# Eight-core decoder layer: inputs and output laid out feature-major by the host, next tile normalised inside the last down projection

## What is computed

```
x = x + 1/2 * SwiGLU_1(RMSNorm(x))          # w1, w3: 1024 x 2816, w2: 2816 x 1024
h = RMSNorm(x); x = x + mixer(h)            # w_in 1024 x 5648, gated linear attention, pooling, merge
x = x + CrossAttention(RMSNorm(x), RMSNorm(mem))
x = x + 1/2 * SwiGLU_2(RMSNorm(x))
out = RMSNorm(x)
rmsnorm(x, g) = x * rsqrt(mean(x*x, axis=-1) + 1e-6) * g
swiglu(h) = (silu(h @ w1) * (h @ w3)) @ w2
```

## Time and profile before

| | us |
|---|---|
| median of 3 runs | 3675.35 (3672.68 to 4205.69) |
| span of the profiled execution, slowest core (core 0) | 3676.3 |
| spans of the eight cores in it | 3661.8 to 3676.3 |
| TensorE matmuls busy | 3382.7 (92%) |
| VectorE, ScalarE, GpSimd busy | 1379.5, 916.6, 353.3 |
| DMA, share of 16 engines | 55.6% (weights), 3.1% (x, mem, out) |

### The profile page before, as it was taken

One profiled execution on the slowest core, in us unless ns is written; L12 is line 12 of the kernel. 1 busy time (PEld: TensorE's weight loads), 2 busy tenths in 40 slices (PEclk: granted clock), 3 DMA queues, 4 the chain that ended last, 5 costly groups with the idle time before them and its releaser, 6 DMA issues.

```text
span 3676.3 us, 43383 instructions; the slowest of 8 cores (3661.8 to 3676.3 us)
## 1 busy us (share of the span) xinstructions
PE 3382.7 (92%) x16248; PEld 1581.1 (43%) x16248; DVE 1379.5 (38%) x1860; ACT 916.6 (25%) x1285; POOL 353.3 (10%) x362
## 2 busy tenths in 40 slices
PE   5999799899799969999979997989998999798998
PEld 3444444344444434334444443434444444343444
DVE  2213545622322354552232246463223125546312
ACT  3112332211311332221131144222113114312211
POOL 1111000011111000001101100001110010000110
PEclk9999899999899979999999998999999999899999
DMA  9568247267766633735875853475595584253565
GB/s 165 69 64 105 39 67 125 36 74 71 112 77 67 85 47 59 126 46 62 83 115 62 81 74 45 73 111 61 63 105 89 66 91 68 36 78 49 69 66 90
DMA packets 538363, 282.33 MB, mean 77 GB/s; under 512 B 261280, under 2 KB 523440, under 8 KB 538160
## 3 DMA queue, kind: packets, MB, share of 16 engines
q0 software_dynamic: 523904, 244.49, 55.6%
q1 hardware_dynamic: 14256, 35.06, 3.1%
HBM read 507.21 MB, written 16.78 MB: 143 GB/s over the span
## 4 chain that ended last, share of the span: by engine, by line
PE 84%; DVE 7%; ACT 3%; issue 2%; DMA 2%; DVEq 0%; POOL 0%; ACTq 0%; SPq 0%; POOLq 0%
PE psum_all L103 84%; DVE sb_hT L378 2%; DVE ov_rz_102 L1056 1%; DMA sb_slot<-xa_wv 1%; DVE ov_rz_103 L1056 1%; DMA out<-ov_ost_51 1%; ACT ov_sq L358 1%; PE psum_all L119 1%; DVE ov_ogT L886 1%; DVE sb_xT L378 1%; DVE ov_xo L1062 1%; ACT ov_rsn L879 0%; ACT ov_rsn L878 0%; ACT ov_osq L868 0%; DVE sb_xT L1010 0%
## 5 line engine op out<-in xcount | busy, mean ns | idle before, releaser
L103 PE MATMUL psum_all<-sb_hT,sb_slot 128*128 128x512 bf16 (+1 forms) x8512 | 1896.6, 385 | 37.3 <-DVE sb_hT L378 30.9
L103 PEld LDWEIGHTS psum_all<-sb_hT,sb_slot 128*128 128x128 bf16 (+1 forms) x8512 | 838.7, 99 | 1060.5 <-issue 99.8
L103 PE MATMUL psum_all<-ov_gated,sb_slot 128*128 128x512 bf16 x2816 | 611.2, 379 | 0.0
L131 POOL DMA_DIRECT2D sb_slot<-ffn_w x264 | 272.3, 1036 | 2099.2 <-PE psum_all L103 2062.4
L103 PEld LDWEIGHTS psum_all<-ov_gated,sb_slot 128*128 128x128 bf16 x2816 | 275.7, 98 | 332.9 <-issue 2.6
L358 ACT ACTIVATE ov_sq<-sb_xT 128x2048 bf16<-128x2048 f32 x80 | 148.4, 1902 | 944.6 <-DVE sb_xT L501 533.1
L486 DVE TENSOR_TENSOR ov_gated<-psum_all,ov_sl_55 128x512 bf16<-128x512 f32 x176 | 121.7, 691 | 478.5 <-PE psum_all L103 478.5
L486 DVE TENSOR_TENSOR ov_gated<-psum_all,ov_sl_54 128x512 bf16<-128x512 f32 x176 | 121.6, 691 | 460.9 <-PE psum_all L103 411.0
L501 DVE SCALAR_TENSOR_TENSOR sb_xT<-psum_all,sb_xT 128x512 f32<-128x512 f32 x128 | 88.1, 691 | 455.5 <-PE psum_all L103 455.5
L378 DVE SCALAR_TENSOR_TENSOR sb_hT<-sb_xT,sb_small,ov_rstd 128x512 bf16<-128x512 f32 x256 | 172.4, 746 | 144.3 <-ACT ov_rstd L372 144.3
L483 ACT ACTIVATE ov_sl_55<-psum_all 128x512 bf16<-128x512 f32 x176 | 105.1, 597 | 487.1 <-PE psum_all L103 487.1
(11 more groups left out here) (174 smaller groups left out, 2292.2 us busy)
## 6 DMA issues: line engine op xcount, KB each, us to landing
sb_slot<-ffn_w POOLq DMA_DIRECT2D x176, 512.0 KB, 8.9
sb_slot<-ffn_w POOLq DMA_DIRECT2D x88, 704.0 KB, 9.4
sb_slot<-w_in POOLq DMA_DIRECT2D x44, 1024.0 KB, 11.8
sb_slot<-w_up_a POOLq DMA_DIRECT2D x8, 1024.0 KB, 8.9
sb_slot<-w_mix_out POOLq DMA_DIRECT2D x8, 1024.0 KB, 12.0
sb_slot<-xa_wq POOLq DMA_DIRECT2D x8, 1024.0 KB, 23.5
sb_slot<-xa_wo POOLq DMA_DIRECT2D x8, 1024.0 KB, 21.4
sb_slot<-w_up_b POOLq DMA_DIRECT2D x4, 1024.0 KB, 9.1
```

Source lines behind the costliest of these rows:

```text
L103: ("ins", (lambda e, o=o, l=l, r=r, st=st, sp=sp: e.matmul(o, l, r, start=st, stop=sp)), i == n - 1)
L131: self.prog[queue].append(("dma", (lambda e, o=o, i=i: e.dma_start(out=o, in_=i)), key))
```

## The change

The host function writes x, mem and out feature-major and each slot's weights in the order in which they lie in the slot, so that a slot load is 128 runs of 4096 float32 (2816 for w2) and x can be read into feature-major buffers directly. All float32 transposes of x, mem and out, `load_block`, `store_block`, `boundary`, `ost`, `stg` and `xpf` go. x is read into two chunk buffers `xin` (58 to 90 K); the first norm reads them and writes `hT`, and phase 2 of ffn(0) takes its residual from them. Stores go from `xT` straight to DRAM. Within phase 2 of ffn(1), hooks run the two first norms of the next tile after groups (0,1), (0,2), (0,4) and (0,5) (chunk, m), and the final norm of chunk 0 after (0,7) and (1,6); the final norm of chunk 1 is deferred into the next tile's phase 1. Squares and multiplications of a norm wait for the groups of features that they read, no longer for all eight. `mem_prologue` moves from the start to between ffn(0) and mixer of the first tile.

```diff
-    x_d = din("x", [SEQ, D])
-    mem_d = din("mem", [MEM, D])
+    x_d = din("x", [SEQ // SUB, 128, 8, SUB])
+    mem_d = din("mem", [128, 8, MEM])
...
+    w13_d = [din("ffn1_w13", [NJ // 2, 128, 4096]), din("ffn2_w13", [NJ // 2, 128, 4096])]
+    w2_d = [din("ffn1_w2", [8, 128, NJ * 128]), din("ffn2_w2", [8, 128, NJ * 128])]
+    win_d = din("w_in", [11, 128, 4096])
...
-        S.dma("pool", [(vf(st), src) for (vf, src) in parts], [], [slot_b[i]], f"dma:slot{i}")
+        S.dma("pool", [(st[:, 0:src.shape[1]], src)], [], [slot_b[i]], f"dma:slot{i}")
...
+    def run_hook(hooks, at):
+        if at in hooks:
+            lab = S.label
+            S.label = lab.split("/")[0] + "/tailnorm"
+            for f in hooks[at]:
+                f()
+            S.label = lab
...
-            S.op("dve", lambda e, bk=bk, m=m, s=s: e.scalar_tensor_tensor(
-                out=xT[:, m, s * SUB:(s + 1) * SUB], in0=bk[:], scalar=0.5, in1=xT[:, m, s * SUB:(s + 1) * SUB],
-                op0=ALU.mult, op1=ALU.add), [bb], [xT_b[m][s]])
+            if x_in is None:
...
+            else:
+                S.op("dve", lambda e, bk=bk, m=m, s=s: e.scalar_tensor_tensor(
+                    out=xT[:, m, s * SUB:(s + 1) * SUB], in0=bk[:], scalar=0.5, in1=x_in[s][0][:, m, :],
+                    op0=ALU.mult, op1=ALU.add), [bb, x_in[s][1][m]], [xT_b[m][s]])
+            run_hook(hooks, (s, m))
...
+    def load_chunk(k, step=4):
+        xt, xb = xin[k % 2]
+        for lo in range(0, 8, step):
+            S.dma("sp", [(xt[:, lo:lo + step, :], x_d[k, :, lo:lo + step, :])], [], xb[lo:lo + step], f"dma:x{k % 2}_{lo}")
+
+    def first_norm(c):
+        xt, xb = xin[c]
+        return norm_pieces(lambda lo, hi: xt[:], lambda c_: xb, T, O_G_FFN1, hdst, hdb, c)
+
+    def final_norm(t, c):
+        p_sq, p_ones, p_rest = norm_pieces(xsrc, xbufs, T, O_G_FIN, xsrc, xbufs, c)
+
+        def p_out():
+            for lo in range(0, 8, 4):
+                S.dma("sp", [(out_d[t * NSUB + c, :, lo:lo + 4, :], xT[:, lo:lo + 4, sl(c)])],
+                      [xT_b[m][c] for m in range(lo, lo + 4)], [], f"dma:out{c}_{lo}")
+        return p_sq, p_ones, p_rest, p_out
...
+    S.label = "load"
+    load_chunk(0, 2)
+    ffn_pre(0)
+    load_chunk(1)
+    n0 = first_norm(0)
+    for p in n0:
+        p()
+    n1 = first_norm(1)
+    n1[0]()
+    deferred.extend(n1[1:])
     for t in range(nt):
...
+        last = t + 1 == nt
+        S.label = "ffn0"
+        if t > 0:
             ffn_pre(0)
...
+        nx = norm_pieces(xsrc, xbufs, T, O_G_MIX, hdst, hdb, 0)
+        ffn(0, xin, {(0, 7): [nx[0]], (1, 6): nx[1:]})
+        if t == 0:
+            mem_prologue()
+        mixer(t)
+        xattn()
+        if not last:
+            load_chunk(2 * t + 2)
+            load_chunk(2 * t + 3)
+        S.label = "ffn1"
+        norm_x_to_h(O_G_FFN2, chunks=(1,))
+        fz = final_norm(t, 0)
+        hooks2 = {(0, 7): [fz[0]], (1, 6): fz[1:]}
+        if not last:
+            na, nb_ = first_norm(0), first_norm(1)
+            hooks2.update({(0, 1): [na[0]], (0, 2): na[1:], (0, 4): [nb_[0]], (0, 5): nb_[1:]})
+        ffn(1, None, hooks2)
+        S.label = "store"
+        fy = final_norm(t, 1)
+        fy[0]()
+        deferred.extend(fy[1:])
+        if last:
+            run_deferred()
```

More of the change, by code:

```diff
@@ L244, in build_program @@
     ptmp, ptmp_b = ov("ptmp", 36, [128, 4, SUB], F32)
-    xpf = [ov(f"xpf{i}", 58 + 4 * i, [128, D], F32) for i in range(8)]
+    xin = [ov(f"xin{i}", 58 + 16 * i, [128, 8, SUB], F32, nb=8) for i in range(2)]
     qT, qT_b = ov("qT", 0, [128, 4, T], BF16, nb=8)
@@ L468, in ffn @@
         for pair in pairs:
-            loaded = [wload(ffn_parts(l, jp), key=("ffn", l, jp)) for jp in pair]
+            loaded = [wload(w13_d[l][jp], key=("ffn", l, jp)) for jp in pair]
             for s in range(NSUB):
@@ L631, in load_tile @@
-    def load_tile(t):
-        S.label = "load"
-        pcs = norm_pieces(xsrc, xbufs, T, O_G_FFN1, hdst, hdb, 0) if stage >= 1 else None
-        for blk in range(T // 128):
-            if pcs is not None and blk == 4:
-                pcs[0]()
-            if pcs is not None and blk == 6:
-                pcs[1]()
-                pcs[2]()
-            load_block(blk)
-    def store_tile(t, final_norm=True):
-        S.label = "store"
-        if final_norm:
-            rmsnorm_T(xsrc, xbufs, T, O_G_FIN, xsrc, xbufs, chunks=(1,), defer_last=True)
-        for blk in range(T // 128):
-            store_block(t, blk)
-            if blk == 1:
-                run_deferred()
@@ L695, in mixer @@
         S.label = "mix"
-        winv = kview(win_d)
-        wpre("mix_q", proj_parts(winv[:, :, 0:512], 4, 8))
-        wpre("mix_k", proj_parts(winv[:, :, 512:1024], 4, 8))
+        wpre("mix_q", win_d[0])
+        wpre("mix_k", win_d[1])
         norm_x_to_h(O_G_MIX, chunks=(1,))
@@ L707, in ev_qk @@
                      [kT_b[s * 4 + i] for i in range(4)])
[L708 to L709 removed]
+        proj_multi([(win_d[0], "mix_q"), (win_d[1], "mix_k")], 4, 8, hrhs, hrb, ev_qk)
+        st, sbuf = wload(wa_d)
         sv = v3(st, 8, 16)
@@ L1070, in ev_o @@
                  [bb], [xT_b[mm_][s]])
-        proj_multi([(wov[:, :, half * 512:(half + 1) * 512], None) for half in range(2)], 4, 8,
+        proj_multi([(wo_d[half], None) for half in range(2)], 4, 8,
                    lambda kc, s: xo[:, kc, sl(s)], lambda s: [xo_b[kc * 2 + s] for kc in range(8)], ev_o,
-                   hook=(tail_hook(O_G_FFN2, 8) if stage >= 4 else None))
-    mem_prologue()
-    prefetch_tile(0)
-    load_tile(0)
+                   hook=tail_hook(O_G_FFN2, 8))
+    S.label = "load"
@@ L1100, in build_program @@
+        ffn(1, None, hooks2)
[5 more added lines that the diff above has]
+            run_deferred()
     fin = []
-    for key in [f"dma:out{i}" for i in range(8)]:
+    for key in [f"dma:out{c}_{lo}" for c in range(2) for lo in (0, 4)]:
         if key in S.dmacnt:
@@ L1147 @@
         m = dict(shared)
-        m["x"] = np.ascontiguousarray(inp["x"][b], dtype=np.float32)
-        m["mem"] = np.ascontiguousarray(inp["mem"][b], dtype=np.float32)
+        m["x"] = np.ascontiguousarray(f32(inp["x"][b]).reshape(SEQ // SUB, SUB, 8, 128).transpose(0, 3, 2, 1))
+        m["mem"] = np.ascontiguousarray(f32(inp["mem"][b]).reshape(MEM, 8, 128).transpose(2, 1, 0))
         in_maps.append(m)
     res = run_bass_kernel_spmd(nc, in_maps, core_ids=list(range(8)))
-    out = np.stack([np.asarray(r["out"], dtype=np.float32) for r in res.results], axis=0)
+    out = np.stack([np.asarray(r["out"], dtype=np.float32).transpose(0, 3, 2, 1).reshape(SEQ, D) for r in res.results],
+                   axis=0)
     return out
```

244 lines of the change are left out of this document (67 added, 177 removed).

## The result

The changed kernel takes **3542.3 us** (median of four runs, 3541.9 to 3543.4) against 3675.35 before: the ratio is 0.9641, 95% interval 0.9625 to 0.9658, 3.6% less. The forecast was 3549 us, 3.4% less. Of four runs of the kernel before, two ran at a lowered clock and are left out of the ratio (3672.68 and 3675.35 us are left).

The account below looks back on a forecast made before the run. TensorE matmuls were taken to bound the kernel, with gains only outside dense runs: 3676.3 - 125.2 (boundaries) - 29.5 (start) + 35 (mem) - 6.3 (end) = 3550.3, taken as 3549 us against the median; range 3525 to 3590.

Parts of the forecast that it names:

- the taking of turns: DMA queues alternate packet by packet whatever the row length, so at the start x chunk 0 lands at 31.5 us.
- the mem term: Between first ffn(0) and mixer: mem load 9.3 us, norm 9.9, K and V matmuls 16.6; +35 us, bounds 28 and 47.
- Boundaries: At the three tile boundaries transposes and waits go and only the layer's matmuls stay: 125.2 us saved together.
- The count "92 matmuls stay": At the first tile boundary only 92 needed matmuls remain, 19.9 of 62.5 us; 89 at the other two, 19.2 us.
- Rival 2: A deferred final norm or norms in phase 2 hold up banks, 12 us each time: 3585 us; chance 10%.
- Start: Before the first dense run: x arrives at 31.5 us, first matmul 43.2, run begins 62.8; 29.5 us saved (20 to 45.6).
- End: After the last final norm, direct stores replace transposes, copies and small stores: 6.3 us saved (2 to 8).
- Weights in slot order: Weight packets fall from 523,904 to about 34,300, queue share to 35%; no gain counted beyond the old prologue.
- "The per-group waits of a norm shorten nothing on TensorE": Norms waiting only for the feature groups they read save nothing, since each chunk-0 norm is early already.
- Rivals 3 and 4: 3: long dense runs lower the clock, near 4050 us, 4%. 4: long rows slow per byte, DMA bound, 3760 us, 3%.

Follow-up runs that it names:

- experiment 5: Changed kernel with the next tile's two first norms put back behind phase 2 of ffn(1): 3593.9 to 3626.5 us, ratio 0.9796.
- Experiments 1 and 2: Changed kernel with x chunk 0 in one DMA of 16 KB rows (lowest 3531.6 us); with the first five weight slot loads in 4 KB rows (3529.7 and 3530.6 us).
- experiment 3: Changed kernel with the first weight slot load waiting until x chunk 0 has landed: 3525.6 to 3526.65 us, ratio 0.9595.
- the six runs of experiment 10: The changed kernel twice and experiments 1, 2, 3 and 5, all with whole weight rows beside mem; mem's last row at 4.6 to 6 us on 21 of 48 cores.
- experiment 6: Kernel before the change with only the weights laid out in slot order: lowest 3679.8 us, ratio 1.0017.
- experiment 7: Changed kernel with the weights back in the reference's order, run twice: ratios 0.9696 and 0.9668, against 0.9639 for the changed kernel beside the second.
- experiments 7 and 8: 8 is the changed kernel with the first slot load behind x chunk 0 and mem loaded and normalised inside ffn(0): lowest 3519.9 us, ratio 0.9573.

## Where the prediction held and where it failed, point by point

The total was 7 us off in 3542, and the sign, the mechanism of the boundaries and the taking of turns held. The step that failed is the mem term, the load of mem above all (+41.5 instead of +35), and that the total was closer than this is luck. Each change below is from core 0 before to core 4 after, the two profiled slowest cores.

- **Boundaries** (forecast -125.2): the stretch from the last evacuation of ffn(1) to the next gate code went from 309.3, 306.6 and 309.8 us to 262.65 three times; phase 2 of ffn(1) grew by 3.5 us for the two groups of column sums. Net -43.2, -40.5, -43.7: **-127.4**. The count "92 matmuls stay" was right to 1.2 us each. Rival 2 has nothing: no wait stands in the boundary, and experiment 5 shows what it costs when the norms are behind (52 us).
- **Start** (-29.5): x at 30.9 us against 31.5, first matmul 43.8 against 43.2, run 64.0 against 62.8: **-28.4**. That the queues take turns by row whatever its length was the disputed step. Experiments 1 and 2 each change the length on one side, and both move the start as the turns say; experiment 3 shows only that the weights beside x are what holds it up. The Trainium skill ("DMA: Bandwidth & Descriptors", section "SWDGE vs HWDGE vs iDMA") has packets of at most 4096 B by preference; the measured mean of 7.4 KB a packet and x at 31 us, not 16, decide against it here. The size was luck, though. The sum had the weights begin at 6 us behind two rows of x an engine, then 30 pairs of 0.851 us. On core 4 the first weight row starts at 7.4 us, when 179 of the 512 rows of x (11 an engine) are gone, and the other 333 take 22 us, some 1.05 us for each of 21 turns: fewer turns, and longer ones. By core, the second Square starts at 26.9 to 32.2 us.
- **mem_prologue** (+35): **+41.5** on the slowest core. This is the step that failed: "Eight pairs of 337 + 683 ns ... less the lead of SP over POOL, 9.3 us". Measured are 15.3 us on core 4. The sum had mem beside V's weights and mix_q alone; K's weights, issued before, were not yet through, so SP's lead is none (the first mem row goes 2.2 us after the issue), and from mem's first to its last row it is 10.6 us with 134 weight rows between, 1.32 us for each of eight pairs instead of 1.02. Where K's weights are through, the load takes 5.3 us and the term is +31 to +33, so the 9.3 us are right for neither form. The pause of TensorE before K is 25.6 us on core 4, where 19 were forecast. In this execution only cores 1 and 4 have the long form; over the six runs of experiment 10, it is 22 cores of 48, and the slowest core is the metric. Norm and matmuls (25.8 us from the Squares to the mixer's first group) were sized at 25.7.
- **End** (-6.3): 20.4 us from the last evacuation against 27.3, **-7.0**.
- **Weights in slot order** (0): right on the old schedule as far as the total can tell (experiment 6), though the start is some 6 us later there. In the new schedule it keeps a slot from being late at the boundaries (experiment 7) and costs at the start; cores 0 to 3, at an equal clock, are if anything slower with it, so that it is worth its price is not shown.
- **"The per-group waits of a norm shorten nothing on TensorE"** is the statement that was wrong. In cross-attention's entry each Square now waits for half of the feature groups, and the time from the first to the last copy of its q falls from 27.6 (27.8 in the last tile) to 25.9 us: 6.9 us together. The column sums before (core 0) and after (core 4):

```profile
609.45 1.89 PE L103 MATMUL psum_all<-ov_sq,sb_onesD 128*128 128x512 bf16 x8 [1.50 <-ACT ov_sq L358]
...
623.50 1.89 PE L103 MATMUL psum_all<-ov_sq,sb_onesD 128*128 128x512 bf16 x8
```

The wait for the Squares is gone. Slot order is not the cause, since experiment 6 still has 27.6 us, and experiments 5 and 7 have 25.9. I had looked at norms with their input long ready, not at those whose input is being evacuated.

- What is left, 6.3 us, lies in the pauses of mixer and attention; before, these differed by up to 12 us from core to core in the same execution, so I ascribe it to nothing.

The sum is 3676.3 - 127.4 - 28.4 + 41.5 - 7.0 - 6.9 - 6.3 = 3541.8, the measured span (the last term is what the others leave). So the total was closer than its terms: mem was 6.5 us too cheap, and 13.2 us of small gains were not foreseen. Rivals 3 and 4: the granted clock is 1.00 in runs with no break across two layers (887 to 1130 us, all eight cores), 0.971 to 0.975 over all, and the weight queue's share is 38.6%, with no wait for an FFN slot. The Trainium skill's current limiter ("TensorE: Matmul & The Clock Gate", Part 1) would have slowed exactly these runs; in the profiled execution of the changed kernel it is not seen with eight cores dense at once. A granted clock of 0.81 is there at times in other executions, as on core 6 in experiment 7.

## What to carry to other kernels

When two queues share the DMA engines, count rows, not bytes: the load that somebody waits for should have rows at least as long as those of the queue beside it, or go alone (one wait on the first weight load was worth 16 us here). Making rows longer for bandwidth's sake was no gain here, where TensorE and not DMA sets the time, and it cost 6 us at the cold start. Look also at what was issued before: here a load takes three times as long on the cores where one issued 14 us earlier is not yet through. Work that is moved off a start should be moved under a dense run with all that it needs (here mem, its norm and V's weights), since removing only the latest of several late inputs gave half of what it seemed to promise.

## What the runs showed of the hardware beyond that

Identical loads issued at the same point of the program came in two lengths by core, 5.3 and about 15 us. With the short one few rows of an earlier weight load were still to go when the load was issued (0 to 14 in the next 3 us), with the long one many (19 to 50), and on cores 0 and 4 of the changed kernel 6 and 134 foreign rows went between. After a pause of 4.7 us the 32 matmuls of V took 9.9 us instead of 6.9, so that wait cost TensorE its own length and some 3 us at a granted clock of 0.51 behind it. And besides 0.5 and 1.00 there are stretches at 0.81 in some executions, seen in the profiled ones of experiments 7 and 8 at the same times on cores 4 and 5 or on cores 6 and 7, while cores 0 to 3 had none.
